# One token block's expert search, decoding and scatter placed ahead of the other's in a fused encoder block

## The reference, cut to what matters

```
q = (xb @ w_query).reshape(TB, PH, 2, 128)            # 8 heads, two halves
s = einsum('thpd,hpkd->thpk', q, sub_keys)            # 128 keys per half
v_half, i_half = top_k(s, 16)
cand = v_half[:, :, 0, :, None] + v_half[:, :, 1, None, :]
cidx = i_half[:, :, 0, :, None] * 128 + i_half[:, :, 1, None, :]
top_s, pos = top_k(cand.reshape(TB, PH, 256), 16)
idx = take_along_axis(cidx.reshape(TB, PH, 256), pos)
g = softmax(top_s)
a = gelu(einsum('td,thkd->thk', xb, expert_u[idx]))
out = einsum('thk,thkd->td', g * a, expert_v[idx])
```

## Time and profile before

| | us |
|---|---|
| median of 3 runs | 1022.85 (1021.88 to 1023.35) |
| profiled execution | 1025.0 |
| its span | 1023.2 |
| TensorE (PE) busy | 987.4 (97%) |
| VectorE (DVE) busy | 759.1 (74%) |
| ScalarE (ACT) busy | 558.7 (55%) |
| GpSimd (POOL) busy | 303.0 (30%) |

### The profile page before, as it was taken

One profiled execution on the slowest core, in us unless ns is written; L12 is line 12 of the kernel. 1 busy time (PEld: TensorE's weight loads), 2 busy tenths in 40 slices (PEclk: granted clock), 3 DMA queues, 4 the chain that ended last, 5 costly groups with the idle time before them and its releaser, 6 DMA issues.

```text
span 1023.2 us, 20535 instructions
## 1 busy us (share of the span) xinstructions
PE 987.4 (97%) x6806; PEld 905.0 (88%) x6806; DVE 759.1 (74%) x1574; ACT 558.7 (55%) x1007; POOL 303.0 (30%) x167
## 2 busy tenths in 40 slices
PE   9999999999999999999999996399999999999997
PEld 9889899899999999999999996278888888888886
DVE  7888868779998876666666662377777777777776
ACT  6456754656545456666666663244444444444444
POOL 0000000267850087787587776200000000000000
PEclk9999999999999999999999999699999999999999
DMA  8767676735677788899888884598887787778782
GB/s 303 242 209 218 185 225 208 245 130 204 207 234 232 234 222 220 222 217 221 218 220 218 222 219 100 163 353 258 258 256 260 260 257 255 255 259 256 260 260 76
DMA packets 129363, 231.77 MB, mean 227 GB/s; under 512 B 30736, under 2 KB 80656, under 8 KB 128912
## 3 DMA queue, kind: packets, MB, share of 16 engines
q1 hardware_dynamic: 110288, 229.86, 70.0%
q0 software_dynamic: 18432, 0.07, 5.4%
q10 hardware_dynamic: 576, 0.93, 0.3%
HBM read 203.47 MB, written 27.33 MB: 226 GB/s over the span
## 4 chain that ended last, share of the span: by engine, by line
PE 63%; POOL 20%; issue 6%; DMA 5%; DVE 3%; ACT 1%; SPq 1%; POOLq 0%; ACTq 0%; DVEq 0%
PE pO L1213 27%; POOL g_scratch L506 20%; PE pTT L1527 16%; PE pM L1527 16%; DMA g_scratch<-held 3%; DMA raw<-in_vrows 1%; PE pSS L1278 1%; DVE wlos L755 1%; PE pSS L1434 1%; DMA xcol<-in_xcol 0%; PE pM L1317 0%; PE pTT L1297 0%; PE pTT L1538 0%; PE pM L1311 0%; DVE gates L956 0%
## 5 line engine op out<-in xcount | busy, mean ns | idle before, releaser
L516 ACT ACTIVATE whis<-raw 128x1024 fp32r<-128x1024 f32 x326 | 344.4, 1057 | 210.0 <-PE pM L1527 168.2
L1213 PE MATMUL pO<-xhi,whis 128*128 128x256 f32 x1008 | 283.6, 281 | 0.0
L1213 PE MATMUL pO<-xhi,wlos 128*128 128x256 f32 x1008 | 281.6, 279 | 0.0
L1213 PE MATMUL pO<-xlo,whis 128*128 128x256 f32 x1008 | 281.6, 279 | 0.0
L506 POOL DMA_INDIRECT g_scratch<-held x128 | 221.6, 1731 | 126.8 <-DVE held L1074 60.2
L1120 DVE TENSOR_TENSOR wlos<-raw,whis 128x1024 fp32r<-128x1024 f32 x125 | 153.2, 1226 | 91.7 <-ACT whis L516 91.7
L755 DVE TENSOR_TENSOR wlos<-raw,whis 128x1024 fp32r<-128x1024 f32 x169 | 205.3, 1220 | 14.8 <-ACT whis L516 14.4
L1213 PEld LDWEIGHTS pO<-xhi,whis 128*128 128x128 f32 x1008 | 189.0, 188 | 2.4 <-issue 2.0
L1213 PEld LDWEIGHTS pO<-xlo,whis 128*128 128x128 f32 x1008 | 189.4, 188 | 0.0
L1213 PEld LDWEIGHTS pO<-xhi,wlos 128*128 128x128 f32 x1008 | 189.0, 187 | 0.0
L491 POOL TENSOR_TENSOR wlos<-raw,whis 128x1024 fp32r<-128x1024 f32 x33 | 80.5, 2444 | 216.2 <-ACT whis L516 216.1
(11 more groups left out here) (257 smaller groups left out, 1711.3 us busy)
## 6 DMA issues: line engine op xcount, KB each, us to landing
raw<-in_stream SPq DMA_DIRECT2D x199, 512.0 KB
raw<-in_vrows SPq DMA_DIRECT2D x128, 512.0 KB
a_scratch<-ast SPq DMA_DIRECT2D x128, 128.0 KB
aring<-a_scratch SPq DMA_DIRECT2D x128, 128.0 KB, 3.1
g_scratch<-ghot SPq DMA_DIRECT2D x32, 256.0 KB, 4.2
held<-g_scratch SPq DMA_DIRECT2D x128, 64.0 KB, 3.0
biasm<-in_bias SPq DMA_DIRECT2D x8, 256.0 KB, 5.7
g_scratch<-held POOLq DMA_INDIRECT x128
```

The costliest lines, as they stand in the source:

```text
L516: act.activation(whi[s], raw[s][:], ACT.Copy).then_inc(hi_ready, 1)
L1213: last = pe.matmul(dst, st, mv, start=(c == 0 and q == 0), stop=(c == len(terms) - 1 and q == 2))
```

## The change

The candidates of both blocks are no longer searched side by side. The loop over `b` encloses everything: sums, search (two heads side by side), subtraction, shifts, decoding, and for block 0 offsets and gates, ahead of block 1's first operation. The low halves that VectorE makes move behind the operations of block 1 (`more_low`), 15 of them up to `routed`, and its wait for GpSimd's last low half moves ahead of block 1's search. ScalarE has two exponentials, behind the gelus of the u tiles 11 and 22. The transposes of the route move to tile 33 and the steps of G to tile 35. Small operands (`first_of`, `keys_of`, `steps16`, `places`, `shifted`) lie in PSUM banks that are free at that time; three copies bring them there. VectorE takes two more low halves (`DVE_FRONT` up to `T_QUERY + 3`), and the product with the sines moves, for the query, from part 0 to part 1 of `rope`, behind the low half of tile 9. `tpad` and `ppad` keep the places of the other tensors.

```diff
-DVE_FRONT = (1, T_QUERY + 1)
+DVE_FRONT = (1, T_QUERY + 3)
-G_FIRST = 39
+G_FIRST = 35
-EXP_AT = 20
-TURN_AT = 37
+EXP_AT = (11, 22)
+TURN_AT = 33
...
-            pool.wait_ge(lo_ready, T_QUERY + 1)
-            for t in range(T_QUERY + 1, T_U + DVE_LO):
+            pool.wait_ge(lo_ready, DVE_FRONT[1])
+            for t in range(DVE_FRONT[1], T_U + DVE_LO):
...
-                if i == EXP_AT:
-                    act.wait_ge(pick_max, 1)
-                    act.activation(route[:, :, 2, :, :], route[:, :, 2, :, :], ACT.Exp).then_inc(pick_exp, 1)
+                if i in EXP_AT:
+                    b = EXP_AT.index(i)
+                    act.wait_ge(pick_max, b + 1)
+                    act.activation(route[:, b, 2], route[:, b, 2], ACT.Exp).then_inc(pick_exp, 1)
...
+                if part == half ^ 1:
                     link(dve.tensor_tensor(turned3, turned3, tables[:, 1, :].unsqueeze(1).to_broadcast([P, HA, T]), ALU.mult))
-                else:
+                if part:
...
+            first_of = pTT[:, 0, :].rearrange("p (b h q k) -> p b h q k", b=TB, q=2, k=TOPK)
+            keys_of = pM[0][:].rearrange("p (b h q k) -> p b h q k", b=TB, q=2, k=TOPK)
+            steps16 = pM[1][:, 0:TOPK]
+            places = pTT[:, 1, 0:2 * PH * TOPK].rearrange("p (s h k) -> p s h k", s=2, h=PH)
+            shifted = pTT[:, 1, 2 * PH * TOPK:4 * PH * TOPK].bitcast(U32).rearrange("p (s h k) -> p s h k", s=2, h=PH)
...
+            dve.tensor_copy(pM[0][:], top_i[:].rearrange("p b h k -> p (b h k)"))
+            dve.tensor_copy(steps16, K("iota16"))
+            link(dve.tensor_copy(pTT[:, 0, :], top_v[:].rearrange("p b h k -> p (b h k)")))
...
+                if b:
+                    dve.wait_ge(lo_ready, T_U + DVE_LO)
+                dve.wait_ge(dve_order, found)
+                for h in range(0, PH, 2):
+                    two = range(h, h + 2)
+                    found = top16_both([pick_v[:, b, x, :] for x in two], [pick_p[:, 0, b, x, :] for x in two],
+                                       [cand[:, b, x, :] for x in two], [candm[:, x - h, :] for x in two])
+                    more_low(b)
+                dve.wait_ge(dve_order, found)
+                dve.tensor_tensor(route[:, b, 2], pick_v[:, b], pick_v[:, b, :, 0:1].to_broadcast([P, PH, TOPK]), ALU.subtract).then_inc(pick_max, 1)
+
+                dve.tensor_scalar(shifted[:, 0], pick_p[:, 0, b], 4, None, ALU.logical_shift_right)
+                link(dve.tensor_scalar(shifted[:, 1], pick_p[:, 0, b], 2, None, ALU.logical_shift_right))
+                dve.tensor_copy(places[:, 0], pick_p[:, 0, b])
+                dve.tensor_copy(places[:, 1], shifted[:, 0])
+                found = mark(dve.tensor_copy(pick_f[:, b], shifted[:, 1]))
+                more_low(b)
...
                 for q in range(2):
...
+                                                   steps16.unsqueeze(1).to_broadcast([P, PH * TOPK, TOPK]), ALU.is_equal))
+                    more_low(b)
                     dve.wait_ge(dve_order, found)
                     found = mark(dve.tensor_tensor(e4, e4, keys_of[:, b, :, q, :].unsqueeze(2).to_broadcast([P, PH, TOPK, TOPK]), ALU.mult))
+                    more_low(2 * b)
                     dve.wait_ge(dve_order, found)
                     found = mark(dve.tensor_reduce(route[:, b, q].rearrange("p h k -> p (h k)"), eq[:], AX_X, ALU.add))
+                    more_low(2 * b)
                     dve.wait_ge(dve_order, found)
                 if b == 0:
                     flat = [route[:, 0, q].rearrange("p h k -> p (h k)") for q in range(2)]
                     link(dve.tensor_scalar(gtmp[:], flat[1], float(P), K("part"), ALU.mult, ALU.add))
                     dve.scalar_tensor_tensor(goff, flat[0], float(NK * P), gtmp[:], ALU.mult, ALU.add).then_inc(offsets_ready, 1)
+                dve.wait_ge(pick_exp, b + 1)
+                link(dve.tensor_reduce(gsum[:, 0, b], route[:, b, 2], AX_X, ALU.add))
+                link(dve.reciprocal(gsum[:, 1, b], gsum[:, 0, b]))
+                share = gsum[:, 1, b].unsqueeze(2).to_broadcast([P, PH, TOPK])
+                if b == 0:
+                    dve.tensor_tensor(gval, route[:, b, 2], share, ALU.mult).then_inc(gates_ready, 1)
+                else:
+                    dve.tensor_tensor(route[:, b, 2], route[:, b, 2], share, ALU.mult).then_inc(routed, 1)
+            more_low(2)
...
             one_hots(0)
             one_hots(1)
-            low_w(at_lo)
+            more_low(T_U + G_FIRST + LO_LEAD - at_lo[0])
```

More of the change, by code:

```diff
@@ L218, in build @@
                 top_i = sbs(router, "top_i", [P, TB, HP, TOPK], U32)
-                top_f = sbs(router, "top_f", [P, TB, HP, TOPK])
+                tpad = sbs(router, "tpad", [P, TB, HP, TOPK])
                 cand = sbs(router, "cand", [P, TB, PH, N_CAND])
@@ L223, in build @@
                 pick_p = sbs(router, "pick_p", [P, 3, TB, PH, TOPK], U32)
-                pick_f = sbs(router, "pick_f", [P, 3, TB, PH, TOPK])
+                pick_f = sbs(router, "pick_f", [P, TB, PH, TOPK])
+                ppad = sbs(router, "ppad", [P, 2, TB, PH, TOPK])
                 pick_x = sbs(router, "pick_x", [P, 2, TB, PH, TOPK])
@@ L1017, in _, with more_low @@
             dve.wait_ge(dve_order, found)
+            split = SHORT_X * TOPK
             pairs = top_v[:].rearrange("p b (h q) k -> p b h q k", q=2)
+            first_of = pTT[:, 0, :].rearrange("p (b h q k) -> p b h q k", b=TB, q=2, k=TOPK)
[3 more added lines that the diff above has]
+            shifted = pTT[:, 1, 2 * PH * TOPK:4 * PH * TOPK].bitcast(U32).rearrange("p (s h k) -> p s h k", s=2, h=PH)
+            e4 = eq[:].rearrange("p (h k) x -> p h k x", h=PH)
+            at_lo = [T_U + DVE_LO]
+            def more_low(n):
+                for _ in range(n):
+                    low_w(at_lo[0])
+                    at_lo[0] += 1
+            dve.tensor_copy(pM[0][:], top_i[:].rearrange("p b h k -> p (b h k)"))
+            dve.tensor_copy(steps16, K("iota16"))
+            link(dve.tensor_copy(pTT[:, 0, :], top_v[:].rearrange("p b h k -> p (b h k)")))
             for b in range(TB):
-                first, second = pairs[:, b, :, 0, :], pairs[:, b, :, 1, :]
-                split = SHORT_X * TOPK
+                first, second = first_of[:, b, :, 0, :], pairs[:, b, :, 1, :]
                 dve.tensor_tensor(cand[:, b, :, 0:split].rearrange("p h (x y) -> p h x y", y=TOPK),
@@ L1028, in _ @@
                                                second[:, :, 0:SHORT_Y].unsqueeze(2).to_broadcast([P, PH, TOPK - SHORT_X, SHORT_Y]), ALU.add))
[L1029 to L1041, removed]
-            low_w(at_lo)
-            dve.wait_ge(dve_order, found)
-            link(dve.scalar_tensor_tensor(pick_x[:, 0], pick_f[:, 2], float(SHORT_X - split // SHORT_Y), pick_f[:, 1], ALU.add, ALU.max))
@@ new lines, in _ @@
+                dve.tensor_scalar(shifted[:, 0], pick_p[:, 0, b], 4, None, ALU.logical_shift_right)
[4 more added lines that the diff above has]
+                more_low(b)
+                dve.wait_ge(dve_order, found)
+                link(dve.scalar_tensor_tensor(pick_x[:, 0, b], pick_f[:, b], float(SHORT_X - split // SHORT_Y), places[:, 1], ALU.add, ALU.max))
@@ L1052, in _ @@
+                link(dve.tensor_scalar(places[:, 1], pick_x[:, 0, b], float(SHORT_Y), float(split - SHORT_X * SHORT_Y), ALU.mult, ALU.add))
+                link(dve.scalar_tensor_tensor(pick_f[:, b], pick_x[:, 0, b], float(TOPK), places[:, 1], ALU.mult, ALU.min))
+                link(dve.tensor_tensor(pick_x[:, 1, b], places[:, 0], pick_f[:, b], ALU.subtract))
                 for q in range(2):
                     found = mark(dve.tensor_tensor(eq[:], pick_x[:, q, b].rearrange("p h k -> p (h k)").unsqueeze(2).to_broadcast([P, PH * TOPK, TOPK]),
-                                                   K("iota16").unsqueeze(1).to_broadcast([P, PH * TOPK, TOPK]), ALU.is_equal))
@@ L1060, in _ @@
                     dve.wait_ge(dve_order, found)
                     found = mark(dve.tensor_reduce(route[:, b, q].rearrange("p h k -> p (h k)"), eq[:], AX_X, ALU.add))
-                    low_w(at_lo + 4)
-                    low_w(at_lo + 5)
+                    more_low(2 * b)
                     dve.wait_ge(dve_order, found)
-                    at_lo += 5
                 if b == 0:
@@ L1129, in next_parts @@
                     v_low(i + LEAD, (s + LEAD) % RING)
-            at_lo += 2
             dve.wait_ge(g_zeroed, 16 * ZERO_PARTS)
```

3 lines of the change are left out of this document (removed).

## The result

| | before | after |
|---|---|---|
| median of 4 runs each, us | 1023.1 (1021.88 to 1028.63) | **999.85** (999.6 to 1000.18) |
| profiled execution | 1025.0 | 999.94 |
| its span | 1023.2 | 998.0 |

The ratio is 0.9763 (95% interval 0.9727 to 0.9798): 2.4% faster, 23.25 us between the medians and 25.06 between the profiled executions. Forecast were 28.5 us and 994.5. In a second set of runs they had 999.65 and 1022.74.

A forecast was written before the change was run, and what follows sets the result against it. The prediction took matmuls to hold most of the chain, with TensorE stopped 23.00 us by late scatters. Gains of 26.5 + 2.4 + 2.6 less 3.0 gave 28.5 us, taken from the median: 994.5 us, range 990.5 to 1001.

The forecast's parts named there:

- rival A: Second block costs more: each operation with PSUM 0.2 us longer, 7 us lost, half clock possible; 1000.5 us, chance 0.14.
- part 1: Change to the v phase: first block decoded first, scatters start 57 us earlier, TensorE's wait and restart go; gain 26.5 us.
- Part 2: Second block, searched and decoded beside VectorE's low halves, delays u tiles 18 to 24; cost 3.0 us, bounds 0.5 and 5.5.
- Part 3: Decoding operands in PSUM: most of the decoding no longer stands for GpSimd, and reading PSUM is not slower.
- Rival E: VectorE reads PSUM at half rate, decoding 12.5 us longer per block, half clock follows; 1031 us, chance 0.03.
- Parts 4 and 5: Ahead of the u phase: two more low halves on VectorE gain 2.4 us, the moved sine product in rope 2.6 us.
- 996.5 if those 2 us lay in the scatters: Time expected if the profiled execution's 2.15 us over the median came from the scatters; otherwise 994.5.
- B: Second block costs nothing, VectorE getting the port ahead of GpSimd, 3 us earlier; 991.5 us, within the forecast's chance of 0.75.
- C: Scatters slow beside a fuller VectorE and the wait returns, from 2.45 us apart; 1001 us at 2.5, chance 0.05.
- D: Scatters don't start earlier because GpSimd waits for something other than the gates; 1021 us, chance 0.03.

The follow-up runs named there:

- scatter_34: Changed kernel with GpSimd also waiting for u tile 33 before the first scatter, so the scatters start about 53 us later: 1020.05 us.
- lo24: Changed kernel with the low halves of u tiles 18 to 23 on GpSimd and VectorE's other nine behind its first product of keys: 996.17 us.
- sbuf: Changed kernel with the decoding's operands back in SBUF in place of PSUM, the order of the blocks kept: 1008.48 us.
- no_front: Changed kernel without its two edits ahead of the u phase (two more low halves on VectorE, sine product moved): 1002.78 us.
- front_only: Kernel before the change with only the two edits ahead of the u phase (low halves and sine product): 1021.04 us, ratio 0.9986.
- lo20: Changed kernel with the low halves of u tiles 18 and 19 on GpSimd, VectorE waiting for them in the second search: 996.0 us.
- rope_undone: Changed kernel with only the sine product put back ahead of tile 9's low half: 1002.95 us.

## Why the prediction was right, and where it was off

The measured 999.85 lies in the stated range of 990.5 to 1001, but 5.35 us over the forecast and outside the 991 to 998.5 that went with its chance of 0.75. It fell into the part of the range that was there for rival A, whose mechanism didn't occur. What was right is the mechanism; that the number still lies in the range is in part luck.

**The bound and part 1.** That the scatters were late because both blocks were decoded ahead of them was right, and so were their start (301 forecast, shifted up to 5 us by the front; 296.5 measured), their last landing (591; 588.1), and the wait gone with a margin (26 us; 32, as SyncE comes to it at 623 and not 617: the load of v tile 1 went out 3 us later than I had it, and the store behind it, which I had overlooked, took the other 3). The walk to the gates was 2.0 us short: they were ready at 295.6 in a trace that is 4.8 us earlier, so at 300.4 and not 298.4, and GpSimd waited 1.1 us for them (296.5 behind a last low half that ended at 295.5). That cost nothing. `scatter_34` shows the wait for the scatters as the cause. The term of 26.5 us is the one **mis-sized**. From the end of the u phase (630.48) to the first product behind v tile 124 (983.35) are 352.9 us, 2.9 more than 125 tiles at 2.80. Before it was 27.1 more (631.75 to 1008.85). The gain is 24.2, since I had left 0.5 for what is late next, with 2 as the bound. Stops of 0.71 and 1.66 us make 2.4 of the 2.9. I had counted TensorE's lead of two tiles and overlooked an order on ScalarE. The chain through the second stop (start, us, what) shows it:

```profile
638.87 0.44 SPq L474
...
639.66 9.89 DMA raw<-in_vrows
...
649.65 0.05 ACT whis L517
...
650.61 0.41 ACT ghi L698
...
651.88 0.28 DVE wfull L1130
652.16 0.29 DVE wfull L1131
652.46 0.35 DVE glo L1136
652.80 0.04 issue
652.85 1.67 PE pTT L1546 x6
```

The load of v tile 8 is issued right behind `gf` and `htok` and takes 9.9 us. ScalarE's rounding of it waits, and queued behind that is `ghi` of tile 7, which TensorE needs one tile earlier. So the lead was one tile shorter than TensorE's own. ScalarE's timeline has the wait, and a smaller one of the same kind ahead of the first stop:

```profile
630.86 1.06 ACT L517 ACTIVATE whis<-raw 128x1024 fp32r<-128x1024 f32 x1 [2.32 <-DMA raw<-in_vrows]
...
649.65 1.06 ACT L517 ACTIVATE whis<-raw 128x1024 fp32r<-128x1024 f32 x1 [5.46 <-DMA raw<-in_vrows]
```

**Part 2.** 3.0 plus 0 to 0.5 forecast, 3.1 and 0.4 measured, at tiles 18 to 25 and 35 as said. One stop of 1.36 us and three short ones make two thirds of it; `lo24` took the 3.1 away.

**Part 3.** Products with an operand in PSUM take 2.29 us as before, and `sbuf` puts the whole move at 8.8 us, which the forecast held only as three operations that still stand. Those three took 2.09, 2.40 and 1.95 us. The Trainium skill, VectorE: DVE Perf Modes, section on the TRN2 errata, has 62 cycles more of fixed cost for a PSUM source. The groups of L1073 and L1077, with one of two operands in PSUM, don't show them against the same products of before from SBUF, L1053 and L1057:

```profile
L1057 DVE TENSOR_TENSOR eq<-eq,top_f 128x2048 f32<-128x2048 f32 x4 | 9.1, 2285 | 0.0
...
L1073 DVE TENSOR_TENSOR eq<-pick_x,pM 128x2048 f32<-128x2048 f32 x4 | 9.1, 2286 | 0.1
L1077 DVE TENSOR_TENSOR eq<-eq,pM 128x2048 f32<-128x2048 f32 x4 | 9.1, 2285 | 0.1
```

The short casts of one operand do show them. Out of PSUM a cast of 128 elements (L1064) takes 282 ns in the changed kernel against 217 from SBUF to SBUF in `sbuf` (L1061), 65 ns more, and a shift that only writes to PSUM (L1060) takes 282 too. I had priced them at 0.28 to 0.3 us, so the sum doesn't suffer. Rival E falls with the products.

**Parts 4 and 5.** 5.0 forecast and 4.79 in the profiles, so the working held for that pair of executions. Taken from the median it was wrong: 1.8 us of it was a stretch of half clock that this one execution had behind its stop, and the experiments put both parts together at 3.1 (`no_front`) or 1.7 (`front_only`). I took one event for the rule.

**From profile to median.** This is the second miss. I took the gain of 28.5 from the profiled execution and from the median alike. The profiled execution of before lay 2.15 over the median of the runs shown then (1.9 over that of the result's four), the one of after 0.1 over its own. So part of the gain, about 1.8 us, was the lateness of one execution. I named the case (996.5 if those 2 us lay in the scatters); the spreads speak for it. The kernels whose end waits for the scatters spread over 3.2 to 7.6 us (before, `front_only`, `scatter_34`, 8 to 13 runs each), those in which they have slack over 0.4 to 3.2 in 4 or 5 runs each, but for the one execution of `lo20`. The granted clock says where the time goes. The 33 runs of the kernel before in the three sets lie between 1019.4 us, with a mean granted clock of 0.988, and 1028.9, with 0.983. Two stretches of half clock at the front, 1.8 us each, can't make 9.5 us. Time in which TensorE waits for the scatters at half clock takes half a us of clock for every us of time, and 0.005 of 1024 us are 5.1 for those 9.5. So, as an estimate from these numbers, most of the spread is a longer or shorter wait for the scatters. How much of the 1.8 us was that, and how much the half clock at the front, isn't shown.

The miss of 5.35 us is then 3.4 in the profiled execution (999.94 against 996.5) and 1.9 in the step to the median. The 3.4 are 2.3 at the change of phase, 0.5 in the second block, 0.2 in the front, and 0.4 in the tail and around the span.

**The rivals.** A would have given 1000.5, close to the measured time, yet by a mechanism that isn't there: the products with PSUM aren't longer, and the short casts are by 0.07 us and not 0.2. The second block didn't cost nothing (B), the scatters slowed down too little to matter (C: 2.30 us apart, 2.45 needed), and they did start earlier (D).

## What to carry to other kernels

When a long serial chain on one queue makes the end late, order the work so that its inputs are ready first, then measure the slack that this leaves; here it was 32 us, and six more low halves for the queue's engine bought 3.1 us with it. Where a stop of many us goes, look at every transfer that falls into the same place, from the first engine that consumes it on, for that is next late. And don't take from the median what one profiled execution had by chance: take the distance of profile and median as part of the range.

## What the runs showed of the hardware

- A stop of 2.1 us on TensorE was followed by half clock in one of two places in the kernel before, in the other place in `no_front`, and not at all in `rope_undone`, which has two (2.08 at 32.63, 2.06 at 636.65), nor in `sbuf` behind 2.03 us at 643.66. Stops of 0.8 to 1.8 us never had it in these profiles; the stop of 7.35 us in `sbuf` did (0.50 in the windows from 305 to 314, in the stop and behind it), and so did those of 19.47 and 23.00.
- VectorE and GpSimd hold each other up in both directions: 2.29 to 4.4 us for VectorE's product, 7.2 to 10.4 us for GpSimd's three low halves. With one of two operands in PSUM neither waits.
- One of two operands in PSUM costs an elementwise product of 2048 elements nothing: 2286 against 2287 ns. A cast of 128 elements out of PSUM takes 282 ns, and 217 from SBUF to SBUF.
